# An accumulating DMA for the low parts of three weight chunks in each seven-product projection, with the read-out of the seven products two chunks earlier

## What is computed

```python
def swiglu_ffn(x, w_gu, w_down):
    gate, up = jnp.split(x @ w_gu, 2, axis=-1)
    return (jax.nn.silu(gate) * up) @ w_down          # w_down: 2816 x 1024

def layer_norm(x, g, b, eps=1e-5):
    xf = x.astype(jnp.float32)
    mu = jnp.mean(xf, -1, keepdims=True)
    var = jnp.mean(jnp.square(xf - mu), -1, keepdims=True)
    return ((xf - mu) * lax.rsqrt(var + eps) * g + b).astype(x.dtype)
```

## Time and profile before

| | us |
|---|---|
| median of 3 runs (range) | 1222.71 (1222.28 to 1223.93) |
| the profiled execution | 1222.66 |
| its span | 1220.9 |
| PE busy | 1207.6 (99%) |
| DVE busy | 881.3 (72%) |
| ACT busy | 664.2 (54%) |

### The profile page before, as it was taken

How to read it: one execution, slowest core, us unless ns; L and a number is a source line. 1 busy time by engine, 2 the same in 40 slices (tenths; PEclk the granted TensorE clock), 3 DMA queues, 4 the chain that set the end, 5 groups by cost and what they waited for, 6 DMA issues and landing times.

```text
span 1220.9 us, 16123 instructions
## 1 busy us (share of the span) xinstructions
PE 1207.6 (99%) x6121; PEld 1015.1 (83%) x6121; DVE 881.3 (72%) x1288; ACT 664.2 (54%) x949; POOL 41.8 (3%) x85
## 2 busy tenths in 40 slices
PE   9999999999999999999999999999999999999997
PEld 7888888888778888888888888888887888888886
DVE  5987755756676666777547677776988777687797
ACT  7565644446666355566436554656553554565561
POOL 2000002100000000000000000000000000000000
PEclk9999999999999999999999999999999999999999
DMA  8676754754545556666547666566565644766652
GB/s 276 198 208 186 249 180 143 244 175 150 152 144 171 182 180 207 191 188 191 202 144 191 190 188 222 170 196 191 173 226 169 186 142 139 227 185 193 189 185 74
DMA packets 152702, 225.83 MB, mean 185 GB/s; under 512 B 8153, under 2 KB 85985, under 8 KB 152625
## 3 DMA queue, kind: packets, MB, share of 16 engines
q1 hardware_dynamic: 150096, 216.10, 56.5%
q0 software_dynamic: 2512, 8.69, 2.7%
q10 hardware_dynamic: 16, 0.00, 0.0%
HBM read 223.72 MB, written 1.05 MB: 184 GB/s over the span
## 4 chain that ended last, share of the span: by engine, by line
PE 93%; DVE 5%; DMA 1%; ACT 1%; issue 0%; SPq 0%; DVEq 0%; ACTq 0%
PE ps L680 23%; PE ps L595 17%; PE ps L602 17%; PE ps L610 17%; PE ps L684 12%; PE ps L520 3%; DVE wl L1770 2%; PE ps L851 1%; DMA raw<-in_moba_w_in_dram 1%; PE ps L864 1%; PE ps L657 1%; PE ps L662 1%; PE ps L660 1%; DMA raw<-in_ff_w_gate_dram 0%; ACT wh L1138 0%
## 5 line engine op out<-in xcount | busy, mean ns | idle before, releaser
L1770 DVE TENSOR_TENSOR wl<-raw,wh 128x1024 fp32r<-128x1024 f32 x405 | 482.2, 1208 | 96.1 <-ACT wh L1138 93.6
L1138 ACT ACTIVATE wh<-raw 128x1024 fp32r<-128x1024 f32 x405 | 413.3, 1042 | 67.5 <-PE ps L610 20.4
L680 PE MATMUL ps<-XT,wh 128*128 128x512 f32 x1216 | 423.0, 394 | 0.0
L684 PE MATMUL ps<-XT,wl 128*128 128x256 f32 x1216 | 338.0, 278 | 0.0
L680 PEld LDWEIGHTS ps<-XT,wh 128*128 128x128 f32 x1216 | 227.9, 187 | 52.3
L684 PEld LDWEIGHTS ps<-XT,wl 128*128 128x128 f32 x1216 | 228.7, 188 | 0.2
L595 PE MATMUL ps<-wh,XT 128*128 128x512 f32 x510 | 203.6, 399 | 0.0
L602 PE MATMUL ps<-wl,XT 128*128 128x512 f32 x510 | 199.5, 391 | 0.3 <-DVE wl L2601 0.3
L610 PE MATMUL ps<-wh,XT 128*128 128x512 f32 x510 | 157.9, 391 | 0.0
L595 PEld LDWEIGHTS ps<-wh,XT 128*128 128x128 f32 x510 | 96.1, 188 | 21.2 <-issue 0.8
L602 PEld LDWEIGHTS ps<-wl,XT 128*128 128x128 f32 x510 | 96.1, 188 | 20.2 <-DVE wl L2601 1.2
(11 more groups left out here) (339 smaller groups left out, 1242.0 us busy)
## 6 DMA issues: line engine op xcount, KB each, us to landing
raw<-in_ffn_w_gu_dram SPq DMA_DIRECT2D x88, 512.0 KB, 4.3
raw<-in_w_in_dram SPq DMA_DIRECT2D x56, 512.0 KB, 4.1
raw<-in_ff_w_up_dram SPq DMA_DIRECT2D x44, 512.0 KB, 4.6
raw<-in_ff_w_down_dram SPq DMA_DIRECT2D x44, 512.0 KB, 4.7
raw<-in_ffn_w_down_dram SPq DMA_DIRECT2D x44, 512.0 KB, 4.6
raw<-in_ff_w_gate_dram SPq DMA_DIRECT2D x40, 512.0 KB, 4.0
raw<-in_gla_w_in_dram SPq DMA_DIRECT2D x24, 512.0 KB, 4.8
raw<-in_moba_w_in_dram SPq DMA_DIRECT2D x24, 512.0 KB, 4.5
```

What stands on the lines that cost most here:

```text
L680: e.matmul(o, wh_of(j)[:, w], XT[:, kt, :, :].rearrange("p a n -> p (a n)"), start=kt == 0, stop=False)
L684: ins = e.matmul(o[:, 0:256], wl_of(j)[:, w], XTH[:, kt, :], start=False, stop=kt == kts - 1)
L1138: e.activation(wh_of(j)[:, 0:m], source(j), ACT.Copy).then_inc(S("wh"), 1)
L1770: e.tensor_tensor(wl_of(j)[:, 0:m], source(j), wh_of(j)[:, 0:m].bitcast(F32), ALU.subtract).then_inc(S("wl"), 1)
```

## The change

1. Chunks 8, 13 and 18 of f3 and of f4 (`others`, six chunks in all) no longer get their low part from DVE. After the high part, ACT writes minus the high part to `wl` (an activation with scale -1), and POOL issues a DMA that adds `raw` to it in place (`low_others`). Its completion (semaphores `wlo0` to `wlo2`) takes the place of DVE's signal, for PE and for the load that reuses the slot of `raw`.
2. ACT's copy for the read-out and DVE's `gather` are called at the step of chunk 22 and not of chunk 23.
3. The three further chunks of lead (`MORE`) in block d0 end three chunks before chunk 22 (`until`). So fewer chunks are prepared ahead of the `gather`, and more behind it.

```diff
+        others = [j for f in SEVEN_FFNS for kind, h, j in mixed[f]
+                  if kind == "eight" and j > mixed[f][4][2] and j < last_seven(f)]
+        def low_done(j):
+            if j in others:
+                i = others.index(j)
+                return S(f"wlo{i % 3}"), 16 * (i // 3 + 1)
+            return S("wl"), j + 1 - len([i for i in others if i < j])
...
             if r >= NR:
-                e.wait_ge(S("wl"), loads[r - NR] + 1)
+                e.wait_ge(*low_done(loads[r - NR]))
...
                     e.activation(wh_of(j)[:, 0:m], source(j), ACT.Copy).then_inc(S("wh"), 1)
+                    if j in others:
+                        e.activation(wl_of(j)[:, 0:m], source(j), ACT.Copy, scale=-1.0).then_inc(S("wn"), 1)
...
-                    high_to(lead(j - 2, further))
+                    high_to(lead(j - 2, further if j < until else 0))
...
-                for t in block(f"{f}d0", 0, MORE if f in SEVEN_FFNS else 0):
+                for t in block(f"{f}d0", 0, MORE, last_seven(f) - 3 if f in SEVEN_FFNS else 0):
...
-                        if f in SEVEN_FFNS and at_chunk["step"] == last_seven(f) + 1:
+                        if f in SEVEN_FFNS and at_chunk["step"] == last_seven(f):
                             e.wait_ge(S("used"), last_seven(f) + 1)
...
                     j = at_chunk["next"]
                     m = chunks[j][1] * chunks[j][2]
+                    at_chunk["next"] += 1
+                    if j in others:
+                        continue
...
+            def low_others(f):
+                for i, j in enumerate(others):
+                    if not blocks[f"{f}d0"][1] <= j < blocks[f"{f}d0"][2]:
+                        continue
+                    e.wait_ge(S("wn"), i + 1)
+                    if i >= 3:
+                        e.wait_ge(*low_done(others[i - 3]))
+                    e.dma_start(wl_of(j), source(j), accum_op=ALU.add).then_inc(low_done(j)[0], 16)
```

More of the change, by code:

```diff
@@ L600, in pe_products @@
                 elif t == 0 and c == 0:
-                    e.wait_ge(S("wl"), j + 1)
+                    e.wait_ge(*low_done(j))
                 e.matmul(o, lh[:, kt, rows(t)], low[:, w], start=False, stop=False)
@@ L658, in pe_seven @@
                     if i == 0:
-                        e.wait_ge(S("wl"), j + c + 1)
+                        e.wait_ge(*low_done(j + c))
                     e.matmul(o, lh, low[:, cols(i)], start=False, stop=False)
@@ L933, in pe_gla @@
             e.wait_ge(S(f"ev{bank_of('low', 0)}"), ev_count["low", 0] - 1)
-            e.wait_ge(S("wl"), at + 1)
+            e.wait_ge(*low_done(at))
             for kt in range(8):
@@ L1142, in more, with block @@
                 high_to(lead(at_chunk["step"] - 1))
-            def block(name, tail=0, further=0):
+            def block(name, tail=0, further=0, until=0):
                 b, at, end, width, kts = blocks[name]
@@ L1747, in weight_sums @@
                 if g:
-                    e.wait_ge(S("wl"), max(i for i in group_of if group_of[i] == (g - 1, 3)) + 1)
+                    e.wait_ge(*low_done(max(i for i in group_of if group_of[i] == (g - 1, 3))))
                 e.wait_ge(*source_ready(j))
@@ L1771, in low_to, with block @@
                                     ALU.subtract).then_inc(S("wl"), 1)
-                    at_chunk["next"] += 1
             def more():
                 low_to(lead(at_chunk["step"] - 1))
-            def block(name, tail=0, further=0):
+            def block(name, tail=0, further=0, until=0):
                 b, at, end, width, kts = blocks[name]
@@ L1782, in block @@
                 for j in range(at, end - tail):
-                    low_to(min(lead(j - 2, further), last))
+                    low_to(min(lead(j - 2, further if j < until else 0), last))
                     at_chunk["step"] = j
@@ L2749, in pool_program @@
                 load_b(ln_b[i, k].partition_broadcast(P))
+                if stage in (6, 8):
+                    low_others("f3" if stage == 6 else "f4")
                 layer_norm(stage)
```

2 lines of the change are left out of this document (1 added, 1 removed).

## The result

The changed kernel takes **1225.88 us** (median of 15 runs, 1223.71 to 1229.09) against 1222.71 us (15 runs, 1220.46 to 1224.40): a ratio of 1.0028, with an interval of 1.0021 to 1.0036. It is slower by 3.2 us where 2.2 us less was forecast. The profiled execution of the changed kernel is the one at the median, 1225.88 us with a span of 1224.2.

The account below looks back on a forecast made before the run. PE, busy 99% of the span, was taken as the bound, with 4.8 us lost at f3's transposes (2.9 wait, 1.9 clock). f3's gain of 3.25 us less f4's loss of 1.03 gave -2.2, 1220.5 us; range 1219.0 to 1227.0.

Parts of the forecast that it names:

- The order: In f3 the gather starts 6.22 us earlier, but four more low parts behind it eat all but 1.67 us.
- the sum of -2.2 us: Whole kernel: f3 gains 3.25 us and f4 loses 1.03 us, giving 1220.5 us.
- the walk: Step-by-step times in f3 from PE's end of chunk 22 to row set 1's transposes at 927.3; chance 0.50.
- a forecast 1.03: PE waits 1.03 us for chunk 29's low part, once in f3 and once in f4.
- the fall of the clock behind the transposes: In f3 before the change, PE's clock at 0.50 for 3.85 us, a loss of 1.93 us.
- the rival of the clock: The clock falls behind the new 1 us waits, up to 1.93 us each, 1222.5 to 1225 us; chance 0.06.
- What the DMA takes off DVE: Three subtractions of 1.14 us pitch leave DVE in each projection, 3.4 us; alone that would remove the 2.9 us wait.
- The unknown T: An addition's time from issue to landing, taken as 5.2 to 5.7 us; free for PE up to 5.75 us.
- the slow DMA: PE waits at chunk 18 from T = 5.75, at 8 from 6.5; chance 0.18 up to T = 6.9, 0.19 above.
- its own rule: Beyond T = 5.75 us PE loses 2 us per us of T in f3 and in f4, 4 us per us.
- its slow side: The range's upper end, 1227.0 us, stood for T near 7.4; some 0.14 lay above it.

Follow-up runs that it names:

- e1: The change with its new order alone and no additions by DMA (DVE makes all low parts): 1220.49 us, 0.9983 of the kernel before.
- e10: The change with additions at chunks 13 and 18 only, DVE making chunk 8: 1228.35 us, 1.0047 of the kernel before.
- e2: The additions at chunks 8, 13 and 18 alone, in the order of the kernel before: 1227.03 us, 1.0034 of that kernel.
- e3: The change with chunk 29's low part ahead of the left half's residuals in f3 and f4: 1225.04 us, 1.0013 of the kernel before.
- e13: A second profile of the unchanged kernel of e2: this execution took 1226.39 us, the first profiled one 1223.69 us.
- e6: The change with plain DMA copies in place of the additions, so the output is wrong: 1220.91 us, 0.9986 of the kernel before.
- e8: The change with additions at chunks 8 and 18 only, DVE making chunk 13: 1220.73 us, 0.9988 of the kernel before.
- e11: The change with the addition at chunk 13 only and chunk 15's load held until chunk 19's may go: 1226.85 us, 1.0028 of the kernel before.
- e4: e1 with chunk 29's low part ahead of the left half's residuals in f3 and f4: 1221.12 us, 0.9985 of the kernel before.
- e9: The change with additions at chunks 8 and 13 only, DVE making chunk 18: 1224.68 us, 1.0010 of the kernel before.

## Why the prediction was wrong

**The order: right, term by term.** The gather (901.56 forecast, 901.51 in e1), the transposes (920.18 and 920.13), those of row set 1 (927.3 and 927.22) and the sum of -2.2 us (-2.1 between the profiled executions) came as the walk had them. Chunk 29 came 0.99 us later than before for a forecast 1.03. One size was off without harm: the fall of the clock behind the transposes was put at 3.85 us and 1.93 us of loss, and the granted clock is 0.83 over 920 to 930 us, a loss of 1.7. The clock stayed at 1.00 behind the waits of the profiled execution, up to 1.72 us, so the rival of the clock did not come true there. Other kernels show that 2 us of wait can bring it (e10).

**What the DMA takes off DVE: wrong.** "By itself that would bring the layer norm 3.4 us forward" holds for DVE's busy time and not for its clock time. e2 has the additions by themselves and its gather is 1.0 us later than before. The walk saw DVE wait some 2 us for the load of chunk 15 and counted that as harmless; measured in f3 of the change are 1.22 us there and 3.79 us at the next group, 5.0 us in all, more than the 3.4 that were saved. And e1 shows that the gather needed none of it.

**The unknown T: here the step failed.** The prediction took one T of 5.2 to 5.7 us for all three additions. The first of each projection took 5.3 and 4.4 us (4.4 was the prediction's estimate for an idle machine), the third 7.5 and 5.3, the second 8.6 and 8.7. With a uniform T it bounded chunks 8 and 18 and did not list chunk 13 at all: PE wanted it at 886.3, 7.1 us after the issue, and no T under 5.75 could touch that. So the sum has nothing for PE's waits at chunk 13, which were 1.52 and 1.71 us. What was missing is that the landing of one addition sets the load under which the next one runs. The text had all the parts: the landing releases loads, "loads in a burst took up to 7.4 us", three loads beside each addition. It used them for the size of T and not for its order in time. "Chunk 8's addition starts when few loads are out" was true, and was no argument for chunk 13's.

**The rival that came nearest** is the slow DMA, at T = 7 with 1225.5 us. Its sign is right. Its size is luck: the median landing was 6.4 us, for which its own rule gives about 1223.1 us. And its place is wrong: the waits are at chunk 13, not at 18. In e10 chunk 18 does become the place.

**How the 5.4 us between the change and e1 are made up** (profiled executions, by how much later the same matmul of PE starts). 0.2 us are there in the first 100 us of the kernel, an accident of this execution. In f3 chunk 13's addition brings 1.8 (the row's 1.52 is counted from a modelled end), and chunk 29 0.9 more, because the gather, and with it the low part of 29 behind it, stands 2.9 us later than in e1 and PE only 2.0. Together 2.9, as the transposes show (923.07 against 920.13). In f4 the addition brings 2.0 and chunk 29 0.2: chunk 29's product stands 5.2 us behind e1's (1208.37 against 1203.20). The last 0.2 us lie behind PE's last matmul, and 0.1 us is spread between the projections.

**The range** of 1219.0 to 1227.0 held the time, 1225.88 us, but only through its slow side, which stood for waits at chunk 18; the forecast itself had the sign wrong, 2.2 us less where 3.2 us more came.

## What to carry to other kernels

A copy or an addition by DMA that holds a buffer also holds the loads queued for that buffer: its landing sends them out together, and the next transfer on which the compute engine waits runs behind them. Give each transfer its own duration from what leaves in the 2 us ahead of it and just behind it, and list the slack of every one, not only of the first and the last. And before paying for relief of an engine, try the reordering alone: here it gave the whole gain.

## What was not expected of the hardware

- An accumulating DMA of 512 KB within SBUF landed in 4.4 to 5.3 us when one load had left some 3.2 us ahead of it, in 5.0 to 6.6 us with two loads of 512 KB, the last 2.2 us ahead, and in 7.3 to 10.1 us when three had left, the last up to 1.6 us ahead or in their midst. Three that left 0.0 to 0.4 us behind it made it take 7.5 to 8.7 us, three from 0.9 us behind on 5.0 to 6.0 us (the change, e2, e3, e13). A plain copy of the same bytes (e6) took 2.8 and 3.7 us at chunk 8 and 8.2 us with a burst.
- The slow addition slowed the loads too: the three loads ahead of it in f3 took 3.6, 6.1 and 7.4 us in the change, and the same three, bunched the same way with no addition behind them, 3.7, 4.6 and 5.4 us in e8.
- The fall of TensorE's clock is not settled by the length of the wait alone. Behind waits of 1.98 (e10, f3), 2.24 (e13) and 2.90 us the granted clock was 0.50 for some 3.4 us; behind 2.02 (e13), 2.15 (e11), 2.38 (e3), 2.74 (e2) and 2.87 us (e10, f4) it stayed at 1.00. Shorter waits had no fall behind them here. A forecast that counts its cost has to give it a chance and not a value.
- A stretch of 93.7 us without a wait took 95.5 us in two of fourteen traces (e3, e4), at a granted clock of 1.00. No run shows why.
- Kernels in which PE waits for additions for over 1 us in all spread over 3.6 to 5.7 us from run to run, the other changed ones over 2.1 to 2.8; the kernel before, which has no additions but the 2.9 us wait, over 3.9 us in 15 runs. A single profiled execution of them can lie 2 to 3.3 us from the median (e2, e3, e9, e11).
